# First attention layer: queries and values projected as one 512-column product and one of 256, keys as three products

## What is computed

```python
def dilated_branch(q, k, v, rel_bias, window, dilation):
    ...
    scores = jnp.where(allowed[:, None], scores + bias, NEG_INF)
    m = jnp.max(scores, axis=-1)
    p = jnp.exp(scores - m[..., None])
    l = jnp.sum(p, axis=-1)
    o = jnp.einsum('bdnhqk,bdnkhc->bdnqhc', p, vv.astype(jnp.float32))
    ...
def reference(x, mem, ...):
    mem_n = rmsnorm(mem, mem_norm)
    for i in range(DEPTH):
        h = rmsnorm(x, mixer_norm[i])
        if i % 2 == 0:
            parts = split_cols(h @ even_w_in[j], [ATTN_W] * N_DIL + [ATTN_W, ATTN_W, CROSS_WIDTH])
            mix = mixer_dilated(parts[:N_DIL], parts[N_DIL], parts[N_DIL + 1], rel_bias)
            qc = parts[N_DIL + 2]
        else:
            ...
            mix = mixer_dsa(q, c_kv, q_idx, k_idx, w_idx, odd_w_uk[j], odd_w_uv[j], rel_bias)
        cross = cross_attention(qc, mem_n, w_mem_kv[i])
        x = x + jnp.concatenate([mix, cross], axis=-1) @ w_out[i]
        h = rmsnorm(x, ffn_norm[i])
        if i % 2 == 0:
            x = x + swiglu(h, even_w_gate[j], even_w_up[j], even_w_down[j])
        else:
            x = x + moe_swiglu(h, odd_w_router[j], odd_w_gate[j], odd_w_up[j], odd_w_down[j])
    return rmsnorm(x, final_norm)
```

## Time and profile before

| | |
|---|---|
| median of 3 runs | 1564.56 us |
| the profiled execution | 1565.14 us |
| its span, first to last instruction | 1563.4 us |
| mean granted TensorE clock | 0.993 |
| TensorE busy | 1527.9 us, 98% |
| VectorE busy | 1326.0 us, 85% |
| ScalarE busy | 1130.7 us, 72% |
| first layer's pairs | about 42 to 210 us of the span |

### The profile page before, as it was taken

One profiled execution on the slowest core, in us unless ns is written; L12 is line 12 of the kernel. 1 busy time (PEld: TensorE's weight loads), 2 busy tenths in 40 slices (PEclk: granted clock), 3 DMA queues, 4 the chain that ended last, 5 costly groups with the idle time before them and its releaser, 6 DMA issues.

```text
span 1563.4 us, 25330 instructions
## 1 busy us (share of the span) xinstructions
PE 1527.9 (98%) x8155; PEld 1288.0 (82%) x8155; DVE 1326.0 (85%) x1806; ACT 1130.7 (72%) x1507; POOL 87.7 (6%) x64
## 2 busy tenths in 40 slices
PE   8899999999999999999999999999999999999997
PEld 7899977888888777888888888888888888888886
DVE  5778868777758878998998998998998998998997
ACT  5565556444446668788878878878878878878875
POOL 1333100000010000000000000000000000000000
PEclk9999999999999999999999999999999999999999
DMA  9844526666623467999999999999999999999992
GB/s 271 216 135 142 159 91 201 189 187 184 167 58 85 145 250 285 409 386 375 381 396 357 396 390 355 393 389 354 390 394 354 388 392 356 392 393 349 404 386 107
DMA packets 226997, 455.38 MB, mean 291 GB/s; under 512 B 12848, under 2 KB 120512, under 8 KB 226944
## 3 DMA queue, kind: packets, MB, share of 16 engines
q1 hardware_dynamic: 222800, 439.52, 77.7%
q0 software_dynamic: 4144, 15.22, 3.9%
HBM read 445.52 MB, written 9.18 MB: 291 GB/s over the span
## 4 chain that ended last, share of the span: by engine, by line
PE 89%; DVE 4%; ACT 3%; DMA 2%; issue 1%; POOL 0%; ACTq 0%; DVEq 0%; POOLq 0%
PE ps L733 25%; PE ps L735 25%; PE ps L734 25%; PE ps L980 5%; PE ps L982 2%; PE ps L1140 2%; DMA big<-in_even_w_in 2%; PE ps L821 1%; ACT w_hi L1178 1%; PE ps L851 1%; DVE w_lo L1525 1%; DVE small L1612 1%; PE ps L836 1%; DVE z L1590 1%; DVE z L1609 1%
## 5 line engine op out<-in xcount | busy, mean ns | idle before, releaser
L1525 DVE TENSOR_TENSOR w_lo<-big,w_hi 128x1024 fp32r<-128x1024 f32 x837 | 983.8, 1214 | 145.2 <-ACT w_hi L1178 69.6
L1438 ACT CAST w_hi<-big 128x1024 fp32r<-128x1024 f32 x672 | 693.6, 1056 | 139.6 <-PE ps L735 136.5
L733 PE MATMUL ps<-w_hi,m_hi 128*128 128x512 f32 (+1 forms) x1008 | 391.9, 389 | 1.5 <-ACT qT L1233 1.3
L735 PE MATMUL ps<-w_hi,m_lo 128*128 128x512 f32 (+1 forms) x1008 | 389.4, 386 | 0.0
L734 PE MATMUL ps<-w_lo,m_hi 128*128 128x512 f32 (+1 forms) x1008 | 389.2, 386 | 0.0
L733 PEld LDWEIGHTS ps<-w_hi,m_hi 128*128 128x128 f32 x1008 | 189.7, 188 | 41.2 <-issue 2.1
L735 PEld LDWEIGHTS ps<-w_hi,m_lo 128*128 128x128 f32 x1008 | 189.6, 188 | 38.3
L734 PEld LDWEIGHTS ps<-w_lo,m_hi 128*128 128x128 f32 x1008 | 189.7, 188 | 37.2
L1178 ACT CAST w_hi<-big 128x1024 fp32r<-128x1024 f32 (+1 forms) x171 | 165.9, 981 | 49.3 <-PE ps L735 36.8
L733 PE MATMUL ps<-w_hi,h_two 128*128 128x512 f32 (+1 forms) x464 | 182.6, 394 | 0.0
L735 PE MATMUL ps<-w_hi,h_two 128*128 128x512 f32 (+1 forms) x464 | 179.9, 388 | 0.0
(11 more groups left out here) (270 smaller groups left out, 1576.0 us busy)
## 6 DMA issues: line engine op xcount, KB each, us to landing
big<-in_odd_w_gate SPq DMA_DIRECT2D x112, 1024.0 KB, 7.3
big<-in_odd_w_up SPq DMA_DIRECT2D x112, 1024.0 KB, 7.4
big<-in_odd_w_down SPq DMA_DIRECT2D x112, 1024.0 KB, 7.5
big<-in_even_w_in SPq DMA_DIRECT2D x42, 512.0 KB, 4.0
big<-in_even_w_gate SPq DMA_DIRECT2D x22, 512.0 KB, 4.6
big<-in_even_w_up SPq DMA_DIRECT2D x22, 512.0 KB, 3.9
big<-in_even_w_down SPq DMA_DIRECT2D x22, 512.0 KB, 4.7
big<-in_w_out SPq DMA_DIRECT2D x20, 512.0 KB, 3.6
```

What stands on the lines that cost most here:

```text
L733: mm(dst, a[0], b[0], start=start, stop=False, **kw)
L735: return mm(dst, a[1], b[0], start=False, stop=stop, **kw)
L1438: nc.scalar.copy(w_hi[:, slot, :], ring[s][:, (u % 2) * UNIT:(u % 2 + 1) * UNIT]).then_inc(s_hi, 1)
L1525: return V.tensor_tensor(dst, src, lead.bitcast(F32), ALU.subtract)
```

## The change

Queries and values of the eight ordinary pairs take the feed-forward's form: for each chunk one product of 512 columns (`w_hi` by both token parts) and one of 256 (`w_lo` by the high part), in a function `wide_product` that the feed-forward now calls too. ScalarE copies the second half of the bank to a small tile `half` (two places in turn), VectorE's new `halves` adds the first half to it and writes `qT` or `vT`. Keys and the cross pairs keep their three products and ScalarE's copy.

`evacuated` now counts VectorE's additions in the first layer (four a pair); the copies of the keys count in `s_keyT`, those of cross queries in `cross_queries`. The waits are written anew with these: the values are turned after VectorE's addition, the scores wait for the keys' copy and for the addition of queries 2, and pair 8's and 9's projections wait until all 32 additions and 8 key copies are done. In VectorE's step the additions stand before low(0), before low(1), after head_probs(now, 1), and after low(4). In `stream` pair 0's additions stand before w_lo of the same matrix of pair 1.

```diff
+        half = XH[:, 0, 0:2 * SEQ].rearrange("p (r n) -> p r n", r=2)
...
-        names = ("evacuated", "turned_v", "values", "scores", "scores_read", "masked", "max", "exp",
+        names = ("evacuated", "cross_queries", "turned_v", "values", "scores", "scores_read", "masked", "max", "exp",
...
+        s_two, s_keyT = sem("two_halves_copied"), sem("even_keys_copied")
...
+        def wide_before(pair, m):
+
+            return pair.value(lambda g: (NBR + 1) * g + (m if m < NBR else NBR))
...
+            def wide_product(dst, w, norm=None):
+
+                for k in range(DC):
+                    if norm is not None:
+                        pe.wait_ge(s_nlo, DC * norm + k + 1)
+                    mm(dst, w[0][:, k, :], h_two[:, k, :, :].rearrange("p s n -> p (s n)"),
+                       start=k == 0, stop=k == DC - 1, skip_group_check=True)
+                    last = mm(dst[:, 0:SEQ], w[1][:, k, :], h_hi[:, k, :], start=False, stop=k == DC - 1,
+                              skip_group_check=True)
+                last.then_inc(s_used, 1)
+
+            def even_bank(pair, m):
+
+                if m == 0:
+                    pe.wait_ge(s_keyT, pair.g)
+                elif m == 1:
+                    pe.wait_ge(s_at[0]["evacuated"], (NBR + 1) * pair.g)
+                else:
+                    pe.wait_ge(s_at[0]["evacuated"], wide_before(pair, m - 2) + 1)
+
             def project(pair, m, norm=None):
                 S = s_at[pair.l]
                 n = pair.before() + m
-                if not (isinstance(n, int) and n < 2):
+                if pair.kind == "even":
+                    if not (isinstance(n, int) and n < 2):
+                        even_bank(pair, m)
+                elif pair.cross and pair.l == 0:
+                    pe.wait_ge(S["evacuated"], (NBR + 1) * PAIRS)
+                    pe.wait_ge(s_keyT, PAIRS)
+                elif pair.cross:
+                    pe.wait_ge(S["evacuated"], 3 * PAIRS)
+                elif not (isinstance(n, int) and n < 2):
                     pe.wait_ge(S["evacuated"], n - 1)
                 if pair.l == 0 and m == 0 and norm is None:
...
+                if pair.kind == "even" and m != pair.nbr:
+                    wide_product(ps[:, pair.bank(m), :], w, norm)
+                    return
                 product(ps[:, pair.bank(m), 0:SEQ], w, src, kc, norm)
...
-                pe.wait_ge(S["evacuated"], pair.before() + pair.mats)
+                pe.wait_ge(S["evacuated"], wide_before(pair, NBR + 1) + 1 if pair.kind == "even" else pair.before() + pair.mats)
...
-                pe.wait_ge(S["evacuated"], pair.before() + (1 if pair.cross else pair.nbr + 1))
+                if pair.cross:
+                    pe.wait_ge(S["cross_queries"], pair.g - PAIRS + 1)
+                elif pair.kind == "even":
+                    pe.wait_ge(s_keyT, pair.g + 1)
+                    pe.wait_ge(S["evacuated"], wide_before(pair, NBR - 1) + 1)
+                else:
+                    pe.wait_ge(S["evacuated"], pair.before() + pair.nbr + 1)
...
-                    pe.wait_ge(s_at[l]["evacuated"], pair_at(l, NPAIR - 1).before() + 1)
+                    pe.wait_ge(s_at[l]["cross_queries"], XPAIRS)
...
+                if pair.kind == "even" and m != pair.nbr:
+                    n = wide_before(pair, m)
+                    if not (isinstance(n, int) and n < 2):
+                        act.wait_ge(S["evacuated"], n - 1)
+                    nc.scalar.copy(half[:, min(m, NBR) % 2, :], ps[:, pair.bank(m), SEQ:2 * SEQ]).then_inc(s_two, 1)
+                    return
...
                 dst = qT[:, pair.par, m, :] if m < pair.nbr else kT[:, pair.par, :] if m == pair.nbr else vT[:, :]
-                nc.scalar.copy(dst, ps[:, pair.bank(m), 0:SEQ]).then_inc(S["evacuated"], 1)
+                done = s_keyT if pair.kind == "even" else S["cross_queries" if pair.cross else "evacuated"]
+                nc.scalar.copy(dst, ps[:, pair.bank(m), 0:SEQ]).then_inc(done, 1)
...
+            def halves(pair, m):
+
+                S = s_at[0]
+                dve.wait_ge(s_two, wide_before(pair, m) + 1)
+                if not (isinstance(pair.g, int) and pair.g < 2):
+                    dve.wait_ge(S["mixed"], 2 * pair.g - 1)
+                if m == NBR + 1 and not (isinstance(pair.g, int) and pair.g < 1):
+                    dve.wait_ge(S["turned_v"], pair.g)
+                dst = qT[:, pair.par, m, :] if m < NBR else vT[:, :]
+                V.tensor_tensor(dst, half[:, min(m, NBR) % 2, :], ps[:, pair.bank(m), 0:SEQ],
+                                ALU.add).then_inc(S["evacuated"], 1)
...
+                def add(m):
+                    if now.gs[-1] < LATE:
+                        halves(nxt, m)
                 if now.kind == "even":
+                    add(0)
                     low(0)
+                    add(1)
                     low(1)
                     head_probs(now, 1)
+                    add(2)
                     low(2)
                     low(3)
...
                 if now.kind == "even":
                     low(4)
+                    add(4)
                 dve.wait_ge(S["mix_hi"], now.g + 1)
                 rest(m_lo[:, bass.ds(now.g, 1), :].rearrange("p o n -> p (o n)"), ps[:, 6, 0:SEQ],
...
                     for m in range(pair_at(l, 1).mats):
+                        if m != NBR:
+                            halves(pair_at(l, 0), m)
                         lo_mat(pair_at(l, 1), m)
```

More of the change, by code:

```diff
@@ L976, in ffn_unit @@
                 bank = (4 if kind == "gate" else 6) + par
-                for k in range(DC):
-                    if norm is not None:
-                        pe.wait_ge(s_nlo, DC * norm + k + 1)
-                    mm(ps[:, bank, :], w[0][:, k, :], h_two[:, k, :, :].rearrange("p s n -> p (s n)"),
-                       start=k == 0, stop=k == DC - 1, skip_group_check=True)
-                    last = mm(ps[:, bank, 0:SEQ], w[1][:, k, :], h_hi[:, k, :], start=False, stop=k == DC - 1,
-                              skip_group_check=True)
-                last.then_inc(s_used, 1)
+                wide_product(ps[:, bank, :], w, norm)
             ffn_unit(0, 0, [0], norm=NORM_FFN0)
```

## The result

The changed kernel takes 1589.38 us, against 1564.55 us for the kernel before: a ratio of 1.016, 95% interval 1.0147 to 1.0174 (four runs of each). It is 24.8 us slower. The prediction said 1576.0, 11.4 us slower. The direction was right and the size less than half of what came, so the question for the experiments was where the other 13 us come from.

What follows compares the result with a forecast made beforehand. TensorE was taken to bound the kernel, with VectorE's order deciding the new waits. Start +2.75, pair 1 +1.4, pairs 2 to 6 +3.6 and pairs 7 and 8 +3.7 gave +11.4: 1576.0 us, range 1570.5 to 1580.5.

Steps and rivals of the forecast that it cites:

- What TensorE gains: Wide units of queries and values: one product fewer per chunk saves 0.07 us a unit, 2.2 us over 32 units.
- The turning of the values: TensorE waits for VectorE's values' addition: period 19.60 instead of 18.88 us, +3.6 in five steps, +1.4 at the first.
- Query 2's addition at no cost: VectorE's addition after the second head's probabilities fits the idle 0.96 us ahead of w_lo of matrix 3, costing nothing.
- from there to where the addition starts: Term of the step's period: from the copy of the keys to the start of VectorE's values' addition, 9.81 us.
- The clock: Rival: after one of two large TensorE waits the clock falls to 1.2 GHz, +1.4 to 1.7 us each; chance 0.13.
- The start: Pair 0's third projection waits 2.9 us for VectorE's first addition, which stands behind five w_lo: +2.75 us.
- rival (a): Half clock after one of the waits at pair 0's third projection and pair 8's: 1577.5 to 1579.5 us, chance 0.13.
- Pair 8: Its projection waits 3.9 us for the last of 32 additions, delaying the turning of pair 7's values: +3.7 us.
- Sum: All delays from the start through pair 8's projection together: +11.4 us, giving 1576.0 us.
- (b): Rival: one of the two large waits, at the start or pair 8, is shorter: 1570 to 1574 us, chance 0.12.
- (c): Rival: not slower, the values' addition covered by ending 1.0 us earlier, with head_scores starting sooner: 1562.4 us, chance 0.12.

## Why the prediction was wrong, point by point

**What TensorE gains.** 0.07 us a unit and 2.2 us were taken; 0.06 and 1.85 (0.9 to 3.9) were measured where TensorE binds. Right. The Trainium skill's rule of N/2.4 GHz + 2.5 ns ("TensorE: Matmul & The Clock Gate", Back-to-back issue gap), by which it would be an estimated 0.6 us, or 0.02 a unit, is not borne out: the periods give 0.05 to 0.07 a unit.

**The turning of the values.** Right in place and mechanism. Where the masks are out of the way, the period behind the first step is 19.58 to 19.71 against 19.60 forecast, and the waits 0.5 to 0.9 us. The terms hold too: with late masks they are 9.33, 9.79 and 0.47 us (turning at 92.09, keys' copy at 101.42, addition at 111.21) for the forecast's 9.23, 9.81 and 0.56. In the changed kernel the addition ends at 112.53 + 0.41 and the turning starts at 113.00, so the semaphore is nearer 0.06 than 0.14.

**Query 2's addition at no cost.** This is the step that failed. The prediction put it into the idle 0.96 us ahead of w_lo of matrix 3, and counted only time. It moved w_lo of matrix 2 by 0.4 us (114.74 in the step of before), from ahead of GpSimd's masks (115.01) to behind their start. Then both w_lo take 4.51 us instead of some 2.5, the gap is full, and 1.34 us come out behind it: the term "from there to where the addition starts", put at 9.81, measured 11.15. With 0.1 us more from the two other terms (9.44 and 0.47 for 9.23 and 0.56), five steps at 21.04 instead of 19.60 are 7.2 us, and the first is 0.2 above its forecast. The prediction had the masks' effect in hand, for the start, and dismissed it for the steps because a w_lo beside masks took 1.26. That row doesn't say that masks do no harm; it says that this order of starts does none. The page of the Trainium skill that it cited ("SBUF — State Buffer", Who interferes with whom) has this too: issue order, not the shape of the operation, decides who blocks. The runs agree: 2.29 us behind a start of GpSimd, 1.22 ahead of it.

**The clock.** Given 0.13 as a rival for two waits near 3 and 4 us. It came in the changed kernel's profile at both, and also after two of the six waits at the turnings, both of about 2 us, for which the prediction had no such term: 1.6 + 1.4 in the steps, 1.25 at pair 8, together 4.3 us between the turnings of pairs 0 and 7. Had the w_lo not been stretched, the waits would have been 0.5 to 0.9 us; after those no drop is seen in the profiles with few or late masks. So this term is mostly the failed step's second half.

**The start.** +2.75 forecast, 3.0 measured by undoing it, +3.5 between the two profiles. The wait is where it was put, and the size is right; that it is right in this profile is partly luck. The third projection was to start at 55.03, 2.9 later than before, and started at 53.15, 1.0 later; the other 2.5 us are rival (a)'s, TensorE at half clock in that projection and the next. The profile with pair 8's wait mended has the forecast's own mechanism: 54.62, 2.5 later, and full clock behind it.

**Pair 8.** A wait of 3.9 forecast, 3.8 found; +3.7 for the step forecast, 23.79 - 18.80 = +5.0 found, the rest being the clock (with the wait filled it is 22.57 - 18.80 = +3.8). Right but for that.

**Sum.** Between pair 0's and pair 7's turning 8.7 us were forecast and 20.5 came. The rest of 11.8 is 7.2 + 0.2 for the steps, 3.0 for the clock in them and 1.25 for it at pair 8, in all 11.7. With the start's 3.5 this is 24.0. Behind pair 7 the changed kernel's profile loses another 3.0 us at half clock, and before's loses 1.8 in the second layer; so the two spans differ by 25.3 us (1588.7 and 1563.4). Neither of these two is shown to be the change's. Rivals (b) and (c) are out: each large wait was there, and the values' addition wasn't covered. What (c) named as the deciding point was right: with the addition inside head_scores the wait was gone.

## What to carry to other kernels

An instruction put into an idle gap costs nothing only if everything behind it in that gap may start later, on its own engine and beside every other one: look at what another engine starts within the gap's width (here GpSimd, 0.27 us behind). A result that another engine waits for goes ahead of work that nobody waits for yet; that one place was worth 17 of 25 us here. And a saving of 1.85 us on the busiest engine, paid with 13 us of work on one that is 81% full, needs every place right only to come out even.

## What the runs showed of the hardware

- A VectorE subtraction of 128x1024 with both operands in SBUF took 1.22 us alone, and 2.29 us when it started 0.06 us behind a GpSimd addition of 128x512. Started 0.27 us ahead of the GpSimd one, it kept its 1.22, and GpSimd's took 2.08 instead of 1.26. GpSimd's three additions took 3.80 us beside head_scores, and 5.5 to 5.7 beside these subtractions, whichever was first: the loss has two payers.
- The granted clock fell to 1.2 GHz after waits of TensorE of about 2 us in an otherwise full stream, but not after each: of the six at the turnings, 1.3 to 2.2 us long, two were hit in the changed kernel's profile and one in each of three others (pair 8's wait, narrow products, the start). Each cost 1.4 to 1.6 us. With unread products in the waits it didn't fall. Which of them is hit was not settled.
- Pairs of products of 512 and 256 columns start 0.350 us apart, three of 256 columns 0.36: fewer and wider products of the same columns give 0.06 us in 2.9.
